# A hybrid decoder step on one core: order of the output projection's halves, and the first FFN run on unnormalised activations

## The chip, the cores and the metric

The kernel runs on one core of a Trainium2 chip. The metric is the device time of one execution in microseconds; the median of three runs is used. The span is what the hardware profiler records from the first instruction to the last. TensorE is called PE in the profile, VectorE DVE, ScalarE ACT, GpSimd POOL; SyncE (SP) issues the weight loads.

## What is computed

Two layers, each a pair of mixers (a Mamba-2 SSD and a Griffin RG-LRU) whose outputs are joined and projected back, followed by a SwiGLU channel mixer: dense in layer 0, eight experts in layer 1. The part that matters here, for 264 tokens (256 of a prompt and 8 samples) and a model width of 1024:

```python
x = x + jnp.concatenate([y_ssd, y_lru], axis=-1) @ P['w_out'][l]
hn = rmsnorm(x, P['ln_ffn'][l])          # x * rsqrt(mean(x*x) + EPS) * g
if l % 2 == 0:
    x = x + (jax.nn.silu(hn @ wg) * (hn @ wu)) @ wd      # D_FF = 2816
else:
    x = x + moe_swiglu(hn, ...)
```

## The kernel before, in words

Activations lie transposed: `xT` and `hn` hold 8 tiles of 128 features by 264 tokens, in f32. The program is written out by hand, one instruction list for each engine, with semaphores between them; nothing is scheduled by a compiler. A PSUM bank carries one output tile at a time. `plan_fills` (line 109) lays down at build time which bank each tile uses and as which fill of it; `begin(name)` on PE waits until the fill before it on that bank has been evicted, `done` counts the bank's `full` semaphore up, `filled` and `evacd` on ACT and DVE are its other side, and `evacuated` waits for an eviction.

Weights come as units of 1 MB (8 k-tiles by 256 columns, which is two output tiles) into a ring of six slots, `wring`. SP issues unit i when unit i-6 has been used. All products of the output projection and of the FFN run in split precision. ACT copies a unit as rounded high part to `fw_hi` (`high_weights`), DVE subtracts that and writes the low part `fw_lo` (`low_weights`, which signals `flo_ready`), and PE makes three products for each k-tile: high by high, low by high, high by low (`split_product`, 24 matmuls for one output tile of 8 k-tiles). There are two slots of `fw` (FSLOTS = 2), so ACT starts the high part of unit j+2 when PE is through with unit j (`unit_used`). The activations are split in the same manner, the mixers' output into `mix_hi` and `mix_lo`, the normalised `hn` into `hn_hi` and `hn_lo`.

The output projection has 8 units a layer, for 4 pairs of output tiles times 2 halves: half 1 multiplies the LRU's output, half 0 the SSD's. OUT_ORDER (line 87) is their order as (pair, half): (0,1), (1,1), (2,1), (0,0), (3,1), (1,0), (2,0), (3,0). I call these steps q0 to q7. A pair's LRU half comes first and opens its banks, its SSD half closes them. The eight output tiles use six banks, OUT_BANKS = (BA, BB, Q1, Q2, Q3, Q4): tiles 6 and 7 (pair 3) take the banks of tiles 0 and 1 (pair 0). In each step ACT waits for the step's unit to be used and makes the high part of the unit two on. DVE makes its low part and then, after an SSD half, adds the two output tiles into `xT` (`add_out`). ACT squares those for the norm (`out_squares`). In the last step DVE adds and ACT squares ahead of the weights.

Then, in both layers: PE sums the squares over the features with a matmul by a constant matrix (`mean_square`, 16 matmul records), ACT takes the square root (`rms`), DVE its reciprocal into `rs[:, 0]` and then x times gain times that (`normed`, 8 instructions), and in layer 0 ACT waits until the memory of the mixers' state is free (`ffn_region_free`), rounds `hn` to `hn_hi` (8 instructions) and DVE subtracts to `hn_lo` (8). The FFN loops over pairs of its 22 tiles, a gate unit (tiles `fg`) and an up unit (tiles `fu`) in turn, all on the two banks BA and BB: ACT evicts `fg` through Silu into `silu_t`, DVE evicts `fu` by multiplying the two into `rs[:, 1:3]`, ACT rounds that to `hid_hi` and DVE subtracts to `hid_lo`. The down projection (`fd`, 8 tiles, 16 units of 704 KB) closes the layer. Layer 1 then goes through the input projections and mixers again, and ends in the router and the experts, which take more than half of the span.

`hn_hi` lies in the memory that holds the low part of the LRU's mixer output, so it may only be written when the last LRU half of the output projection is done.

Of the kernel before, what the change touches and what calls it, by code (L numbers as in the profile page):

```python
# [23 lines left out]
F32 = mybir.dt.float32  # L24
# [8 lines left out]
KD = D // P  # L33
# [53 lines left out]
OUT_ORDER = ((0, 1), (1, 1), (2, 1), (0, 0), (3, 1), (1, 0), (2, 0), (3, 0))  # L87
# [23 lines left out]
def plan_fills():  # L111
# [12 lines left out]
    for l in range(LAYERS):  # L124
# [54 lines left out]
        if l == 0:  # L179
            for m in range(0, FT, 2):  # L180
                for kind in ("fg", "fu"):
                    for i in range(2):
                        tile(kind, m + i)
            for m in range(KD):
                tile("fd", m)
# [72 lines left out]
def trunk(nc, a, o):  # L258

    with ExitStack() as ctx:  # L260
# [233 lines left out]
        copies_out = sem("copies_out")  # L494
        hid_hi_ready = sem("hid_hi_ready")
# [339 lines left out]
        def _(pe):  # L835
# [154 lines left out]
            for l in range(LAYERS):  # L990
# [120 lines left out]
                for q, (pair, lru) in enumerate(OUT_ORDER):  # L1111
# [11 lines left out]
                    if lru:  # L1123
                        ins.then_inc(half_used, 1)
                mean_square(("ln_ffn", l), mean_d[:, :], [sq[:, m] for m in range(KD)],
                            lambda i: pe.wait_ge(sq_ready, 16 * l + 8 + i + 1))
                if l == 0:
                    for m in range(0, FT, 2):
                        for q, kind in enumerate(("fg", "fu")):
                            for i in range(2):  # L1130
# [4 lines left out]
                                     kind, m + i)  # L1135
                    for m in range(KD):
# [156 lines left out]
        def _(act):  # L1293
# [30 lines left out]
            for l in range(LAYERS):  # L1324
# [135 lines left out]
                for q, j in enumerate(OUT[l]):  # L1460
# [7 lines left out]

                    if q == len(OUT[l]) - 1:
                        out_squares()  # L1470
# [3 lines left out]
                    if not lru and q < len(OUT[l]) - 1:  # L1474
                        out_squares()
                    if q == 0:
                        high_parts(0, 4, XT)
                rms(("ln_ffn", l), 0)
                if l == 0:
                    ffn_region_free(act)  # L1480
                    for k in range(KD):
                        act.wait_ge(hn_ready, 8 + k + 1)
                        f(hn_hi[:, k], hn[:, k]).then_inc(hn_hi_ready, 1)
                    for i, j in enumerate(FFN):
                        w, last = UNITS[SPLIT[j]][0], UNITS[SPLIT[j]][5]
                        if w == "ffn_w_gate":
                            for m in (last[1] - 1, last[1]):
                                if m > 1:
                                    evacuated("fu", m - 2)
                                evacd(f(silu_t[:, m % 2, :], filled("fg", m)[:, 0:T], ACT.Silu), "fg", m)  # L1490
                        if i + FSLOTS < len(FFN):
                            unit_used(act, j)
                            high_weights(j + FSLOTS)
                        if w == "ffn_w_up":
                            for m in (last[1] - 1, last[1]):
                                evacuated("fu", m)
                                f(hid_hi[:, m, :], rs[:, 1 + m % 2, :]).then_inc(hid_hi_ready, 1)
# [103 lines left out]
        def _(dve):  # L1601
# [131 lines left out]
            for l in range(LAYERS):  # L1733
# [173 lines left out]
                for q, j in enumerate(OUT[l]):  # L1907
                    pair, lru = OUT_ORDER[q]

                    def add_out():  # L1910

                        for m in (2 * pair, 2 * pair + 1):
                            evacd(tt(xT[:, m, :], xT[:, m, :], filled("out", l, m)[:, 0:T], ALU.add), "out", l, m)

                    if q == len(OUT[l]) - 1:
                        add_out()
                    if j + FSLOTS < len(SPLIT):
                        low_weights(j + FSLOTS)
                    if not lru and q < len(OUT[l]) - 1:
                        add_out()  # L1920
                    if q == 0:
                        norm_parts(("ssd_norm", l, 1), 1, ysz, "ssd_norm", 4, XT)
                        low_parts(0, 4, XT)
                normed(("ln_ffn", l), l, "ln_ffn")
                if l == 0:
                    for k in range(KD):
                        dve.wait_ge(hn_hi_ready, k + 1)
                        tt(hn_lo[:, k], hn[:, k], hn_hi[:, k].bitcast(F32), ALU.subtract).then_inc(hn_lo_ready, 1)
                    for i, j in enumerate(FFN):
                        w, last = UNITS[SPLIT[j]][0], UNITS[SPLIT[j]][5]  # L1930
                        if w == "ffn_w_up":
                            for m in (last[1] - 1, last[1]):
                                evacuated("fg", m)
                                if m > 1:
                                    dve.wait_ge(hid_lo_ready, m - 1)
                                tt(rs[:, 1 + m % 2, :], silu_t[:, m % 2, :], filled("fu", m)[:, 0:T], ALU.mult
                                   ).then_inc(evac[fill("fu", m)[0]], 1)
# [207 lines left out]
```

## Time and profile before

| | us |
|---|---|
| median of 3 runs | 1835.09 (1833.96 to 1836.92) |
| the profiled execution | 1836.94 |
| its span | 1835.2 |
| PE busy | 1741.7 (95%) |
| DVE busy | 1356.3 (74%) |
| ACT busy | 1053.7 (57%) |
| PE's granted clock, mean | 0.976 |

The profiled execution's own time is 1.74 us more than its span. PE is the busiest engine and carries 83% of the chain that ended last. In the 40 slices of the page the stretches that matter here are slices 5 to 11 (layer 0's output projection from 223 us, its FFN from 289 to 488 us) and slices 16 and 17 (layer 1's output projection from 688 to 745 us). In a line of the timeline stand the start, the time taken, the engine, line, operation, names and count, and in brackets how long the engine was idle before it and who released it. Matmul ends are modelled and overlap the next start, so the step from one matmul to the next is read from starts. In a line of the stretches stand its bounds, its length, the busy time of PE, PEld (the weight load into PE), DVE, ACT and POOL, each with its count of instructions, and then the granted clock (1.00 is the level of 2.4 GHz, 0.50 that of 1.2 GHz), the DMA engines' busy share and GB/s.

### The profile page before, as it was taken

How to read it: one execution, taken by the hardware profiler on the slowest of the kernel's cores; microseconds unless marked ns; L12 is line 12 of the kernel's file. 1: busy time of each engine (PE TensorE's matmuls, PEld its weight loads, DVE VectorE, ACT ScalarE, POOL GpSimd, SP SyncE). 2: the span in 40 equal slices, each digit the busy share in tenths (PEclk: the TensorE clock that was granted, in tenths of full speed). 3: DMA queues.
4: the chain of work that ended last, by engine and by line, in shares of the span. 5: the costliest groups of instructions: out<-in, count | busy, mean ns of one | idle time of the engine just before them, and what ended most of it. 6: DMA issues, size and time to landing. Idle time of an engine off the chain costs nothing.

```text
span 1835.2 us, 24108 instructions
## 1 busy us (share of the span) xinstructions
PE 1741.7 (95%) x9024; PEld 1459.8 (80%) x9024; DVE 1356.3 (74%) x1335; ACT 1053.7 (57%) x1006; POOL 139.6 (8%) x135
## 2 busy tenths in 40 slices
PE   7999889999999988799999999999999999999995
PEld 5867788999887768778878788788788788787884
DVE  3668745554456775478888888888888888888885
ACT  2535434443242543366677776767776767776764
POOL 2056000000105420000000000000000000000000
PEclk9999999999999999799999999999999999999998
DMA  8455244555635425279999899899899899998991
GB/s 243 138 182 175 81 152 139 182 149 168 200 119 184 153 89 163 79 285 357 322 353 357 311 365 355 317 358 351 322 359 349 326 355 321 353 358 310 363 357 43
DMA packets 257028, 465.45 MB, mean 254 GB/s; under 512 B 8493, under 2 KB 108197, under 8 KB 256929
## 3 DMA queue, kind: packets, MB, share of 16 engines
q1 hardware_dynamic: 250288, 442.20, 69.9%
q0 software_dynamic: 6384, 21.28, 3.4%
q8 instruction: 42, 0.69, 0.2%
q10 hardware_dynamic: 288, 1.08, 0.2%
q14 instruction: 26, 0.21, 0.0%
HBM read 453.70 MB, written 11.15 MB: 253 GB/s over the span
## 4 chain that ended last, share of the span: by engine, by line
PE 83%; DVE 10%; ACT 2%; issue 2%; POOL 2%; DMA 1%; DVEq 0%; ACTq 0%; POOLq 0%
PE bank L851 80%; PE bank L855 2%; DVE arena L1624 2%; DVE arena L1627 2%; DVE w_lo L1627 1%; DVE moe_arena L1624 1%; ACT fw_hi L1307 1%; DVE fw_lo L1627 1%; DVE cs_t L1627 1%; ACT arena L1307 1%; DMA arena<-in_state_ssd 1%; POOL sam_tmp L740 1%; DVE arena L1829 0%; ACT w_hi L1307 0%; POOL sam_tmp L731 0%
## 5 line engine op out<-in xcount | busy, mean ns | idle before, releaser
L1627 DVE TENSOR_TENSOR w_lo<-wring,w_hi 128x2048 fp32r<-128x2048 f32 x336 | 768.3, 2291 | 118.0 <-ACT w_hi L1307 117.0
L1307 ACT ACTIVATE w_hi<-wring 128x2048 fp32r<-128x2048 f32 x336 | 643.6, 1918 | 254.3 <-PE bank L851 254.2
L851 PE MATMUL bank<-w_hi,xg_hi 128*128 128x512 f32 x896 | 359.8, 402 | 10.7 <-DVE w_lo L1627 9.0
L851 PE MATMUL bank<-w_lo,xg_hi 128*128 128x512 f32 x896 | 355.1, 396 | 0.0
L851 PE MATMUL bank<-w_hi,xg_lo 128*128 128x512 f32 x896 | 352.4, 393 | 0.0
L851 PE MATMUL bank<-hn,wring 128*128 128x264 f32 x1152 | 271.2, 393 | 6.2 <-DVE hn L1624 6.1
L851 PEld LDWEIGHTS bank<-hn,wring 128*128 128x128 f32 x1152 | 220.3, 193 | 50.2 <-issue 12.1
L1627 DVE TENSOR_TENSOR fw_lo<-wring,fw_hi 128x2048 fp32r<-128x2048 f32 (+1 forms) x54 | 113.1, 2095 | 132.8 <-ACT fw_hi L1307 132.8
L851 PEld LDWEIGHTS bank<-w_hi,xg_hi 128*128 128x128 f32 x896 | 168.3, 188 | 51.1 <-DVE w_lo L1627 12.6
L851 PEld LDWEIGHTS bank<-w_lo,xg_hi 128*128 128x128 f32 x896 | 168.2, 188 | 41.0
L851 PEld LDWEIGHTS bank<-w_hi,xg_lo 128*128 128x128 f32 x896 | 168.4, 188 | 38.7
L851 PE MATMUL bank<-w_hi,at_hi 128*128 128x512 f32 x448 | 178.4, 398 | 0.0
L851 PE MATMUL bank<-w_lo,at_hi 128*128 128x512 f32 x448 | 177.0, 395 | 0.0
L851 PE MATMUL bank<-w_hi,at_lo 128*128 128x512 f32 x448 | 175.9, 393 | 0.0
L1307 ACT ACTIVATE fw_hi<-wring 128x2048 fp32r<-128x2048 f32 (+1 forms) x54 | 94.9, 1758 | 111.7 <-PE bank L851 111.7
L1307 ACT ACTIVATE arena<-bank 128x11 f32<-128x11 f32 (+4 forms) x96 | 31.9, 349 | 177.5 <-PE bank L851 169.5
L1624 DVE SCALAR_TENSOR_TENSOR arena<-bank,par,arena 128x255 f32<-128x255 f32 (+2 forms) x120 | 57.6, 481 | 64.2 <-ACT arena L1307 61.2
L851 PEld LDWEIGHTS bank<-w_lo,at_hi 128*128 128x128 f32 x448 | 84.1, 188 | 21.1
L851 PEld LDWEIGHTS bank<-w_hi,at_lo 128*128 128x128 f32 x448 | 84.1, 188 | 20.2
L851 PEld LDWEIGHTS bank<-w_hi,at_hi 128*128 128x128 f32 x448 | 84.1, 188 | 19.2
L851 PE MATMUL bank<-hn_hi,fw_hi 128*128 128x264 f32 x352 | 88.5, 287 | 4.4 <-ACT hn_hi L1307 4.4
L851 PE MATMUL bank<-hn_hi,fw_lo 128*128 128x264 f32 x352 | 88.4, 286 | 0.0
(237 smaller groups left out, 2118.7 us busy)
## 6 DMA issues: line engine op xcount, KB each, us to landing
wring<-in_moe_w_gate SPq DMA_DIRECT2D x112, 1024.0 KB, 5.2
wring<-in_moe_w_up SPq DMA_DIRECT2D x112, 1024.0 KB, 5.2
wring<-in_moe_w_down SPq DMA_DIRECT2D x112, 1024.0 KB, 5.0
wring<-in_w_in SPq DMA_DIRECT2D x36, 1024.0 KB, 5.2
wring<-in_w_out SPq DMA_DIRECT2D x16, 1024.0 KB, 5.4
wring<-in_ffn_w_gate SPq DMA_DIRECT2D x11, 1024.0 KB, 5.4
wring<-in_ffn_w_up SPq DMA_DIRECT2D x11, 1024.0 KB, 5.3
wring<-in_ffn_w_down SPq DMA_DIRECT2D x16, 704.0 KB, 4.7
```

The costliest lines, as they stand in the source:

```text
L740: nc.gpsimd.tensor_tensor(prod, st, sam_c, ALU.mult).then_inc(prod_ready, 1)
L851: return nc.tensor.matmul(out, lhsT, rhs, start=start, stop=stop)
L855: return nc.tensor.transpose(out, in_, ident[0:k, 0:k])
L1307: return nc.scalar.activation(out, in_, fn, **kw)
L1624: return V.scalar_tensor_tensor(out=out, in0=in0, scalar=scalar, in1=in1, op0=op0, op1=op1)
L1627: return V.tensor_tensor(out, in0, in1, op)
```

## The change

Three edits. In both layers the order of the projection's steps q4 and q5 is exchanged: the SSD half of pair 1 now comes before the LRU half of pair 3. In layer 0 the FFN's gate and up products are fed with x times the norm's gain, without the division by the root mean square; that division is applied to each gate and up tile as DVE evicts it. In layer 0 the tiles of the FFN use the six banks in turn rather than two.

In detail, for layer 0: right behind each `add_out` DVE writes `hn` = xT times gain for the two tiles (8 `tensor_scalar` in place of 8 `scalar_tensor_tensor` behind the norm). ACT rounds them in pairs (`scaled_high`): pairs 0 and 1 in step (3,1), behind the weights and `ffn_region_free`; pair 2 in step (2,0); pair 3 in the last step ahead of the squares. DVE subtracts (`scaled_low`) pairs 0 and 1 in step (2,0), pair 2 in the last step ahead of its adds, pair 3 behind them. PE's `mean_square` stands behind the first gate tile. DVE evicts `fg` and `fu` with a multiplication by `rs[:, 0]`, ACT applies Silu in place in `silu_t`, and DVE multiplies the two. ACT makes the weights' high part ahead of its Silu rather than behind it. Layer 1 keeps its norm as it was.

The diff, without the new semaphores' declarations:

```diff
-OUT_ORDER = ((0, 1), (1, 1), (2, 1), (0, 0), (3, 1), (1, 0), (2, 0), (3, 0))
+OUT_ORDER = ((0, 1), (1, 1), (2, 1), (0, 0), (1, 0), (3, 1), (2, 0), (3, 0))
@@ plan_fills
             for m in range(0, FT, 2):
-                for kind in ("fg", "fu"):
+                for k, kind in enumerate(("fg", "fu")):
                     for i in range(2):
-                        tile(kind, m + i)
+                        pl.add(OUT_BANKS[(2 * m + 2 * k + i) % 6], kind, m + i)
             for m in range(KD):
-                tile("fd", m)
+                pl.add(OUT_BANKS[m % 6], "fd", m)
@@ tensor
-                mean_square(("ln_ffn", l), mean_d[:, :], [sq[:, m] for m in range(KD)],
-                            lambda i: pe.wait_ge(sq_ready, 16 * l + 8 + i + 1))
+                def ln_ffn():
+                    mean_square(("ln_ffn", l), mean_d[:, :], [sq[:, m] for m in range(KD)],
+                                lambda i: pe.wait_ge(sq_ready, 16 * l + 8 + i + 1))
+                if l == 1:
+                    ln_ffn()
...
                                 done(split_product(begin(kind, m + i), FFN[m + q], 0, KD, hn_hi, hn_lo, i * P, hi, ready),
                                      kind, m + i)
+                                if first:
+                                    ln_ffn()
@@ scalar
+                    def scaled_high(pair):
+                        for k in (2 * pair, 2 * pair + 1):
+                            act.wait_ge(hn_ready, 8 + k + 1)
+                            f(hn_hi[:, k], hn[:, k]).then_inc(hn_hi_ready, 1)
                     if q == len(OUT[l]) - 1:
+                        if l == 0:
+                            scaled_high(3)
                         out_squares()
                     if j + FSLOTS < len(SPLIT):
                         unit_used(act, j)
                         high_weights(j + FSLOTS)
                     if not lru and q < len(OUT[l]) - 1:
                         out_squares()
+                    if l == 0 and OUT_ORDER[q] == (3, 1):
+                        ffn_region_free(act)
+                        scaled_high(0)
+                        scaled_high(1)
+                    if l == 0 and OUT_ORDER[q] == (2, 0):
+                        scaled_high(2)
...
                 if l == 0:
-                    ffn_region_free(act)
-                    for k in range(KD):
-                        act.wait_ge(hn_ready, 8 + k + 1)
-                        f(hn_hi[:, k], hn[:, k]).then_inc(hn_hi_ready, 1)
                     for i, j in enumerate(FFN):
-                        if w == "ffn_w_gate":
-                            for m in (last[1] - 1, last[1]):
-                                if m > 1:
-                                    evacuated("fu", m - 2)
-                                evacd(f(silu_t[:, m % 2, :], filled("fg", m)[:, 0:T], ACT.Silu), "fg", m)
                         if i + FSLOTS < len(FFN):
                             unit_used(act, j)
                             high_weights(j + FSLOTS)
+                        if w == "ffn_w_gate":
+                            for m in (last[1] - 1, last[1]):
+                                evacuated("fg", m)
+                                f(silu_t[:, m % 2, :], silu_t[:, m % 2, :], ACT.Silu).then_inc(silu_ready, 1)
                         if w == "ffn_w_up":
-                                evacuated("fu", m)
+                                act.wait_ge(hid_ready, m + 1)
                                 f(hid_hi[:, m, :], rs[:, 1 + m % 2, :]).then_inc(hid_hi_ready, 1)
@@ vector, in add_out behind the two adds
+                        if l == 0:
+                            for m in (2 * pair, 2 * pair + 1):
+                                evacuated("out", l, m)
+                                V.tensor_scalar(hn[:, m, :], xT[:, m, :], col(l, PA, "ln_ffn", m), None, ALU.mult
+                                                ).then_inc(hn_ready, 1)
+                    def scaled_low(pair):
+                        for k in (2 * pair, 2 * pair + 1):
+                            dve.wait_ge(hn_hi_ready, k + 1)
+                            tt(hn_lo[:, k], hn[:, k], hn_hi[:, k].bitcast(F32), ALU.subtract).then_inc(hn_lo_ready, 1)
                     if q == len(OUT[l]) - 1:
+                        if l == 0:
+                            scaled_low(2)
                         add_out()
+                        if l == 0:
+                            scaled_low(3)
...
+                    if l == 0 and OUT_ORDER[q] == (2, 0):
+                        scaled_low(0)
+                        scaled_low(1)
...
-                normed(("ln_ffn", l), l, "ln_ffn")
+                if l == 1:
+                    normed(("ln_ffn", l), l, "ln_ffn")
                 if l == 0:
-                    for k in range(KD):
-                        dve.wait_ge(hn_hi_ready, k + 1)
-                        tt(hn_lo[:, k], hn[:, k], hn_hi[:, k].bitcast(F32), ALU.subtract).then_inc(hn_lo_ready, 1)
+                    evacuated("ln_ffn", l)
+                    link(V.reciprocal(rs[:, 0, :], rs[:, 0, :]))
                     for i, j in enumerate(FFN):
+                        if w == "ffn_w_gate":
+                            for m in (last[1] - 1, last[1]):
+                                if m > 1:
+                                    dve.wait_ge(hid_ready, m - 1)
+                                evacd(tt(silu_t[:, m % 2, :], filled("fg", m)[:, 0:T], rs[:, 0, :], ALU.mult), "fg", m)
                         if w == "ffn_w_up":
                             for m in (last[1] - 1, last[1]):
-                                evacuated("fg", m)
                                 if m > 1:
                                     dve.wait_ge(hid_lo_ready, m - 1)
-                                tt(rs[:, 1 + m % 2, :], silu_t[:, m % 2, :], filled("fu", m)[:, 0:T], ALU.mult
-                                   ).then_inc(evac[fill("fu", m)[0]], 1)
+                                evacd(tt(rs[:, 1 + m % 2, :], filled("fu", m)[:, 0:T], rs[:, 0, :], ALU.mult), "fu", m)
+                            for m in (last[1] - 1, last[1]):
+                                evacuated("fu", m)
+                                dve.wait_ge(silu_ready, m + 1)
+                                tt(rs[:, 1 + m % 2, :], rs[:, 1 + m % 2, :], silu_t[:, m % 2, :], ALU.mult
+                                   ).then_inc(hid_ready, 1)
```

## Rows read from the trace of the kernel before

**Rows 1.** The page of the kernel before: span, busy time and instructions of each engine

```profile
span 1835.2 us, 24108 instructions
...
PE 1741.7 (95%) x9024; PEld 1459.8 (80%) x9024; DVE 1356.3 (74%) x1335; ACT 1053.7 (57%) x1006; POOL 139.6 (8%) x135
```

**Rows 2.** Waits of PE, 223 to 289 us: in total, times, longest

```profile
PE bank L851 <- DVE xT L1627: 4.7, 1, 4.7
...
PE bank L851 <- ACT hn_hi L1307: 4.4, 1, 4.4
...
PE bank L851 <- DVE fw_lo L1627: 1.0, 1, 1.0
```

**Rows 3.** Timeline of PE, layer 0, steps q3 to q5

```profile
244.05 0.39 PE L851 MATMUL bank<-mix_hi,fw_hi 128*128 128x264 f32 x1 [1.04 <-DVE fw_lo L1627]
...
249.04 1.16 PE L851 MATMUL bank<-mix_lo,fw_hi 128*128 128x264 f32 x8
...
254.86 0.59 PE L851 MATMUL bank<-mix_hi,fw_hi 128*128 128x264 f32 x1 [4.67 <-DVE xT L1627]
...
260.31 0.31 PE L851 MATMUL bank<-mix_hi,fw_hi 128*128 128x264 f32 x1
```

**Rows 4.** Timeline of ACT, layer 0

```profile
250.23 1.91 ACT L1307 ACTIVATE fw_hi<-wring 128x2048 fp32r<-128x2048 f32 x1 [5.26 <-PE bank L851]
...
288.40 3.17 ACT L1307 ACTIVATE hn_hi<-hn 128x264 fp32r<-128x264 f32 x8 [3.33 <-DVE hn L1624]
...
303.41 1.92 ACT L1307 ACTIVATE fw_hi<-wring 128x2048 fp32r<-128x2048 f32 x1 [3.65 <-PE bank L851]
```

**Rows 5.** Timeline of DVE, layer 0

```profile
252.18 2.29 DVE L1627 TENSOR_TENSOR fw_lo<-wring,fw_hi 128x2048 fp32r<-128x2048 f32 x1 [4.88 <-ACT fw_hi L1307]
...
254.38 0.76 DVE L1627 TENSOR_TENSOR xT<-xT,bank 128x264 f32<-128x264 f32 x2
...
285.95 1.80 DVE L1667 RECIPROCAL rs<-rs 128x264 f32<-128x264 f32 x1
...
305.37 2.29 DVE L1627 TENSOR_TENSOR fw_lo<-wring,fw_hi 128x2048 fp32r<-128x2048 f32 x1 [1.45 <-ACT fw_hi L1307]
```

**Rows 6.** Timeline of PE, layer 0, from the norm to the second unit

```profile
280.82 3.72 PE L851 MATMUL bank<-arena,mean_d 128*128 128x264 f32 x16
...
288.96 0.56 PE L851 MATMUL bank<-hn_hi,fw_hi 128*128 128x264 f32 x1 [4.42 <-ACT hn_hi L1307]
...
297.36 0.28 PE L851 MATMUL bank<-hn_hi,fw_hi 128*128 128x264 f32 x1
```

**Rows 7.** Timeline of PE, layer 1, steps q3 to q5

```profile
713.83 1.16 PE L851 MATMUL bank<-mix_lo,fw_hi 128*128 128x264 f32 x8
...
719.65 0.59 PE L851 MATMUL bank<-mix_hi,fw_hi 128*128 128x264 f32 x1 [4.66 <-DVE xT L1627]
...
724.86 0.28 PE L851 MATMUL bank<-mix_hi,fw_hi 128*128 128x264 f32 x1
```

**Rows 8.** One line's instructions (L1752): duration in ns min/median/max, starts

```profile
L1752 DVE TENSOR_SCALAR dts<-dts,a_neg x2: 345/346/346, 58.1 to 524.7; 16x264 f32<-16x264 f32 x2
```

**Rows 9.** Timeline of POOL, its last transfer of layer 0's mixers

```profile
208.12 0.52 POOL L812 DMA_DIRECT2D out<-arena  x1
```

**Rows 10.** Busy time by stretch; behind POOL stand granted clock, DMA share, GB/s

```profile
250.10:260.20 10.10, 5.43 (x25) 5.34 (x25) 2.97 (x3) 2.68 (x3) 0.00 (x0) 0.67 0.52 172
...
289.00:298.00 9.00, 9.00 (x54) 9.00 (x55) 4.86 (x14) 4.68 (x11) 0.00 (x0) 0.70 0.19 66
...
493.00:494.00 1.00, 1.00 (x4) 0.79 (x3) 1.00 (x3) 0.00 (x0) 0.00 (x0) 0.50 0.83 340
...
786.00:788.00 2.00, 1.90 (x8) 1.58 (x9) 1.82 (x2) 0.00 (x0) 0.00 (x0) 1.00 0.95 379
```

**Rows 11.** Timeline of PE, two other gaps

```profile
491.52 8.82 PE L851 MATMUL bank<-hn,wring 128*128 128x264 f32 x31 [3.03 <-DVE hn L1624]
...
786.10 0.49 PE L851 MATMUL bank<-w_hi,xg_hi 128*128 128x512 f32 x1 [1.56 <-DVE xg_lo L1627]
```

More of the change, by code:

```diff
@@ L494, in trunk @@
         copies_out = sem("copies_out")
+        silu_ready = sem("silu_ready")
+        hid_ready = sem("hid_ready")
         hid_hi_ready = sem("hid_hi_ready")
```

## Prediction, written before the changed kernel ran

> **What bounds the kernel now.** First the page: PE is busy for 1741.7 of 1835.2 us [rows 1], so only PE's gaps and its slow stretches can be won, and an edit to ACT or DVE counts only where PE waits for it. Next the waits of PE around the changed code, 223 to 289 us. There are three: 4.7 us for DVE's add into `xT`, 4.4 us for ACT's `hn_hi`, and 1.0 us for a low part of weights [rows 2]. The timelines then show each gap and what follows it.
>
> The first gap: step q3 ends with eight matmuls from 249.04 that take 1.16 us, so PE could go on at about 250.02 by the step between starts, but it begins q4 at 254.86 [rows 3]. q4 was (3,1). Its tile 6 lies in the bank of tile 0, and tile 0 is evicted late, because DVE makes the low part of the next weights ahead of its adds. ACT starts the high part at 250.23, when the unit is used [rows 4], DVE the low part at 252.18, the adds at 254.38 [rows 5], and PE starts 0.05 us behind the first add's end. After the gap PE's granted clock is 0.50: the stretch from 250.10 to 260.20 has a mean of 0.67 [rows 10], and q4's first tile takes 260.31 - 254.86 = 5.45 us [rows 3]. A tile at full clock takes (280.82 - 260.31) / 7 = 2.93 us [rows 3, 6].
>
> The second gap: the norm's 16 matmul records run from 280.82 for 3.72 us; then PE waits 4.42 us, while ACT takes the root, DVE the reciprocal (1.80 us) and the first `hn`, and ACT the first `hn_hi` [rows 4 to 6]. PE starts the FFN at 288.96, and again behind a gap the clock is low, 0.70 over 289 to 298 us [rows 10]. The first up tile starts at 297.36 [rows 6].
>
> Layer 1 has the first gap once more: q3's last eight from 713.83, q4 at 719.65, its second tile at 724.86 [rows 7].
>
> **The exchanged order, both layers.** In the new order q4 is (1,0), whose banks are open and whose weights had been split during q2; PE waits for nothing. q5 is (3,1) and starts two tiles later, at 250.02 + 5.86 = 255.88. Tiles 0 and 1 are added by 254.38 + 0.76 = 255.14 [rows 5], 0.7 us before, and tile 0 already at 254.8. The weights of (3,1), made at 252.18 to 254.47, are ready as well. Later steps keep the old pattern: unit used, 1.91 us of ACT, 2.29 us of DVE, together with the hand-overs 4.45 us of the 5.86 us that a unit takes on PE. So no new wait follows. SP issues the two exchanged weight units in the other order, six units ahead; nothing is queued differently behind them, and POOL's list is untouched.
> Gain in layer 0: 254.86 - 250.02 = 4.84 us of gap and 5.45 - 2.93 = 2.52 us of slow clock, 7.36 us. In layer 1: free at 713.83 + 0.98 = 714.81, so 4.84 us, and 724.86 - 719.65 - 2.93 = 2.28 us; 7.12 us. The wait of 1.04 us ahead of q3 [rows 3] stays in both layers.
>
> **The norm behind the first gate tile, layer 0.** What is taken off PE's path is root, reciprocal and the gain's multiplication. What becomes late next is the last pair's add, since PE now wants `hn_hi` right behind q7. I follow it from PE's clock: q4 at 250.02, q5 at 255.88, q6 at 261.74, q7 at 267.60, all products done at 273.46.
> ACT learns that q6's unit is used about 0.2 us behind (250.23 against 250.02), so it makes the high part from 267.80 to 269.71, DVE the low part from 269.75, and the adds of pair 2 start 2.20 us later, at 271.95. From here DVE has a queue: two adds (step 0.34 us, from 0.76 us for two with 0.42 us for the last), two `tensor_scalar`, four subtractions of pairs 0 and 1, two of pair 2, then the add of tile 6. No row shows `tensor_scalar` on 128x264 from SBUF. The nearest is 346 ns for 264 elements with a pointer scalar [rows 8], on 16 partitions; overlapped like the others it is a step of 0.26 us. Its bounds are that and the add's 0.34 us step. I take 0.26. The sum is 2 x 0.34 + 2 x 0.26 + 6 x 0.34 = 3.24 us, so tile 6 is added from 275.2 to 275.65, and its bank, the first gate tile's, is free at 275.70. PE idles from about 273.6 to 275.70, 2.1 us; counted in starts the gap is 275.70 - 273.46 = 2.24 us (2.5 at the upper bound).
> The Trainium skill, "VectorE: DVE Perf Modes", section "The perf-mode tier table", has fp32 `tensor_scalar` from SBUF at twice the rate of `tensor_tensor`; the row of 346 ns beside 0.42 us agrees. Without that mode the gap would be the 2.5 us.
> ACT squares pair 2 and rounds it in time: eight roundings take 3.17 us [rows 4], 0.40 us each, behind two squares that take about as long each. Then tiles 6 and 7: `tensor_scalar` done at 276.25 and 276.5, `hn_hi` at 276.7 and 277.1, `hn_lo` at 277.2 and 277.6. PE asks for k-tile 6 of the high part 1.5 us after its start, at 277.2, and for the low parts at 277.7: no second wait, with 0.1 to 0.5 us to spare. Squares of tiles 6 and 7 end at 277.8, ahead of the norm's turn at 275.70 + 2.93 = 278.6. ACT's `ffn_region_free` now stands at 263.9 instead of behind the norm. It waits for transfers of which the last was issued at 208.12 [rows 9]; it costs nothing.
> PE's path from 250.02 to the first up tile is then 8 tiles of the projection (23.44), the gap (2.24), two gate tiles (5.86) and the norm (3.72): 35.26 us. Before it was 297.36 - 250.02 = 47.34 us. Gain 12.08 us, of which the exchange was 7.36 and the norm's move is 4.72: its gap goes from 4.42 to 2.24, and a slow start of 2.5 us goes.
>
> **Behind that, in the FFN.** The root ends at about 283, the reciprocal at 285, when the second gate tile is still on PE (it ends at 285.3). The gate tiles wait for eviction until then, which is what the six banks are for: PE may run six tiles before it needs BA again. ACT needs 1.3 us more for loading Silu's table, behind its weights; the first product is asked for four tiles later.
> In the steady loop DVE gets two more multiplications of 0.43 us per pair of tiles and kind, 44 in all, 19 us of work. They stand ahead of `fw_lo` in its list, so they count only if they are late. Before, ACT starts the up unit's high part at 303.41 and DVE the low part at 305.37, to 307.66 [rows 4, 5]; PE wants it at 297.36 + 4 x 2.93 = 309.08. So there is 1.4 us to spare, and about 2.0 us in which DVE waits for ACT anyway. The new work in front is the second `fu` eviction and two products behind it, with their waits 1.5 us: less than 2.0, cost nothing. ACT's Silu moves behind its weights and gives the gate unit's 0.3 us more. The down projection starts on BA, whose last gate or up tile (20) is evicted one tile before.
>
> **The sum.** 12.1 + 7.1 = 19.2 us. From the profiled execution's span 1835.2 this is 1816.0, with the 1.74 us around it 1817.7. The median of the runs stands 1.85 us below the profiled execution, so 1835.1 - 19.2 = 1815.9. I say 1816.0.
>
> **Rivals.**
> The clock falls in the new gap. The rows leave it open: an idle time of 3.03 us was followed by the low level (0.50 at 493 us), after 1.56 us it stayed at 1.00, and 2.1 us lies between [rows 10, 11]. PE had worked densely before both. A tile lost 2.3 to 2.5 us behind the old gaps [rows 3, 7]; a shorter stretch may cost half of it. So 1.2 to 2.5 us: 1817.2 to 1818.5. I give it 0.22, as the new gap is nearer to the short one.
> DVE's queue around q7 is longer than worked out, by its own hand-overs and by waits between ACT and DVE in turn (DVE waits for ACT's rounding of pair 2, ACT for DVE's products). Then the norm's move wins nothing, with a gap of over 4 us and a slow start as before, and only the exchange pays, 14.5 us: 1820.6. 0.08.
> Slower than before: the FFN becomes bound by DVE. The Trainium skill, same page, section "Rules for kernel authors", advises keeping the count of DVE operations small, and this change adds some 44. The mechanism here is `fw_lo` of the up unit held behind evictions and products. It decides from 2.0 + 1.4 = 3.4 us of DVE work behind the unit's end, against 1.5 us worked out. To turn 19 us into a loss, each of 11 pairs must lose over 1.7 us more, that is 5.1 us of DVE work in all; with 5.6 us the loss is 11 x 2.2 = 24 us, 1840. Against it: DVE idles 1.45 us even ahead of `fw_lo` now [rows 5]. 0.03.
> The exchange does not do what it says: PE waits at (3,1) or at another bank for as long as before, and the norm's new place only moves the 4.4 us. Then 1833 to 1836, no change. 0.03.
> The other side of the clock: slow stretches that follow later gaps (layer 1's start, the router) fall otherwise, as the places of PE's gaps shift in time. Each is worth up to 2.5 us either way; with two gained, below 1812.5. 0.04.
> The remaining 0.60 is the forecast, 1814 to 1817.5.
>
> **Range and chances.** 1812.5 to 1821.5 takes in the forecast, the fall of the clock and the lost norm move. About 0.2% (3.7 us) is what a measurement of this kernel can tell from no change. Faster by more: 0.60 + 0.22 + 0.08 + 0.04 = 0.94. Same 0.03, slower 0.03.
>
> **What would show it.** In the trace after: no idle time of PE between q3 and q7 in either layer, with full clock; a gap of about 2.1 us behind q7 of layer 0, released by DVE's add into `xT`; the norm's matmuls behind 24 of the FFN's and no wait behind them; no idle time of PE in the FFN; the first up tile 35 us behind q3's end. I am wrong if PE waits for `fw_lo` in the FFN, if the gap behind q7 is over 3 us, or if layer 1 gains less than 6 us.

## The result, and the profile after

The changed kernel takes 1819.39 us (median of 4 runs, 1817.82 to 1821.73), the kernel before 1835.49 in the same comparison. The ratio is 0.991, 95% interval 0.9897 to 0.9924: faster by 14 to 19 us. In a second comparison, beside 15 runs of the kernel before, it was 1818.98 and 0.9903 (0.9888 to 0.9918). The profiled execution took 1819.49 with a span of 1817.8 us. The forecast was 1816.0 with a range of 1812.5 to 1821.5.

From the page of the kernel after, to be held against [rows 1]: PE has 7 us less busy time for the same 9024 matmuls, nearly all of it in the two changed stretches, where it ran at the low clock less often. DVE has 15 us more, and the rest of the saving, 10 us, is idle time of PE that went.

```profile
span 1817.8 us, 24173 instructions
...
PE 1734.5 (95%) x9024; PEld 1453.0 (80%) x9024; DVE 1371.3 (75%) x1379; ACT 1052.1 (58%) x1006; POOL 139.5 (8%) x135
```

The waits of PE from 220 to 290 us. In [rows 2] there were three; the 4.7 us and the 4.4 us are gone, 1.0 us ahead of q3 stays, and 2.1 us is the new wait for the last pair's add:

```profile
PE bank L853 <- DVE xT L1645: 2.1, 1, 2.1
PE bank L853 <- DVE fw_lo L1645: 1.0, 1, 1.0
```

The timeline of PE, kernel after: q3 of layer 0, the first gate tile, the norm, the first up tile, layer 1's first projection, and in layer 1 q3 and the router's first matmul. They answer to [rows 3], [rows 6], [rows 7] and the first line of [rows 11].

```profile
243.13 0.39 PE L853 MATMUL bank<-mix_hi,fw_hi 128*128 128x264 f32 x1 [1.04 <-DVE fw_lo L1645]
...
274.79 0.39 PE L853 MATMUL bank<-hn_hi,fw_hi 128*128 128x264 f32 x1 [2.10 <-DVE xT L1645]
...
277.84 3.72 PE L853 MATMUL bank<-arena,mean_d 128*128 128x264 f32 x16
...
284.36 0.28 PE L853 MATMUL bank<-hn_hi,fw_hi 128*128 128x264 f32 x1
...
478.51 8.76 PE L853 MATMUL bank<-hn,wring 128*128 128x264 f32 x32 [3.03 <-DVE hn L1642]
...
697.33 0.39 PE L853 MATMUL bank<-mix_hi,fw_hi 128*128 128x264 f32 x1 [1.04 <-DVE fw_lo L1645]
...
736.27 10.38 PE L853 MATMUL bank<-w_router,hn 128*128 128x8 f32 x48 [5.82 <-issue]
```

Read from q3's start to the first up tile: 284.36 - 243.13 = 41.23 us, before 297.36 - 244.05 = 53.31 [rows 3, 6]. That is 12.08 us less. The DVE list that sets the new wait, which answers to [rows 5]:

```profile
268.83 2.29 DVE L1645 TENSOR_TENSOR fw_lo<-wring,fw_hi 128x2048 fp32r<-128x2048 f32 x1 [3.56 <-ACT fw_hi L1316]
271.04 0.76 DVE L1645 TENSOR_TENSOR xT<-xT,bank 128x264 f32<-128x264 f32 x2
271.72 0.62 DVE L1935 TENSOR_SCALAR hn<-xT,par 128x264 f32<-128x264 f32 x2
272.25 2.14 DVE L1645 TENSOR_TENSOR hn_lo<-hn,hn_hi 128x264 fp32r<-128x264 f32 x6
274.31 0.76 DVE L1645 TENSOR_TENSOR xT<-xT,bank 128x264 f32<-128x264 f32 x2
```

The first of the last two adds ends at 274.74 and PE starts at 274.79. PE's products of q7 ended about 272.7, when DVE had only just begun (at 272.25) with the six subtractions of `hn_lo` that stand ahead of the add.

A table of stretches, from starts of PE's matmuls in eight traces (us). "Before again" is a second trace of the kernel before; the others are the experiments below.

| trace | start to q3 | q3 to layer 1's first matmul | to q3 of layer 1 | to the router | to the end |
|---|---|---|---|---|---|
| before | 244.05 | 247.47 | 217.34 | 46.02 | 1080.32 |
| before again | 243.72 | 247.48 | 217.18 | 46.12 | 1080.40 |
| after | 243.13 | 235.38 | 218.82 | 38.94 | 1081.53 |
| after again | 245.64 | 235.36 | 218.91 | 38.94 | 1081.45 |
| order only | 241.98 | 240.37 | 217.54 | 38.94 | 1080.67 |
| norm only | 241.92 | 244.30 | 219.73 | 46.41 | 1081.14 |
| sum ahead | 241.59 | 234.36 | 219.67 | 38.94 | 1081.64 |
| adds first | 242.17 | 233.30 | 217.36 | 38.94 | 1081.53 |

The second and fourth column hold the changed code. After against before they give 12.1 and 7.1 us, 19.2 in all. The spans differ by 17.4: 0.9 us came ahead of q3, where the traces of unchanged code scatter from 241.59 to 245.64, 1.5 us was lost in layer 1's mixers and 1.2 us in the rest, in code that was not changed.

### The profile page after: what moved, and what is told of

Same layout as the page of the kernel before. It is cut to its first block, busy times and chain, and to the rows that moved or that the text cites. A ratio compares the mean times of both kernels' runs of the same rounds, so it can differ in the third digit from the quotient of the medians.

```text
span 1817.8 us, 24173 instructions
## 1 busy us (share of the span) xinstructions
PE 1734.5 (95%) x9024; PEld 1453.0 (80%) x9024; DVE 1371.3 (75%) x1379; ACT 1052.1 (58%) x1006; POOL 139.5 (8%) x135
## 4 chain that ended last, share of the span: by engine, by line
PE 83%; DVE 10%; ACT 2%; issue 2%; POOL 2%; DMA 1%; DVEq 0%; ACTq 0%; POOLq 0%
PE bank L853 81%; PE bank L857 2%; DVE arena L1642 2%; DVE arena L1645 2%; DVE w_lo L1645 1%; DVE moe_arena L1642 1%; DVE fw_lo L1645 1%; DVE cs_t L1645 1%; DMA arena<-in_state_ssd 1%; ACT fw_hi L1316 1%; ACT arena L1316 1%; POOL sam_tmp L742 1%; DVE arena L1847 0%; POOL sam_tmp L733 0%; DVE arena L1872 0%
```

## Experiments

**The changed kernel again, and the kernel before again.** No edit.

> The changed kernel once more, beside the kernel before on one chip. In the first pair of profiles the steps that the change touches gave 12.1 us in layer 0 and 7.1 us in layer 1, 19.2 us in all, but the spans differ by 17.4 us and the medians by 16.1 us. Theory: the rest is lost in code that was not changed, by slow stretches of PE's clock behind gaps that both kernels have, and that is chance; then the difference of medians over more runs lies between 16 and 19.5 us, and the two changed stretches again give 12.1 and 7.1 us. Rival: the changed kernel loses 2 to 3 us systematically in the unchanged stages; then the difference stays at 16 us with little scatter and the same stages lose again.

Measured: 1818.98 us against 1836.36. In the trace the changed stretches are the same to 0.02 us (table), and layer 1's mixers take 218.91 us. Both comparisons together, eight runs of the changed kernel have a mean of 1819.5; 15 of the kernel before have 1836.0. The difference is 16.5 us, at the low end of what the theory of chance allowed, and the mixers lost the same 1.5 us again, as the rival had it. This run doesn't tell the two apart.

> The kernel before once more, for a second trace of it. Measured from the first matmul of layer 1's input projection to step q3 of layer 1, code that no kernel here changes, the kernel before took 217.3 us and the order-only kernel 217.5 us, and the kernels with the norm's move 217.4 to 221.7 us, mostly 218.8 and more. Theory of chance: it depends on where PE's slow stretches fall, and the kernel before can give 219 to 220 us as well. Theory of a systematic loss: it is 217.3 to 217.6 us again.

Measured: 1836.58 us in its one run, and 217.18 us in layer 1's mixers, as the theory of a systematic loss had it. The trace of the padded kernel below speaks against it.

**Only the order.**

```diff
-OUT_ORDER = ((0, 1), (1, 1), (2, 1), (0, 0), (3, 1), (1, 0), (2, 0), (3, 0))
+OUT_ORDER = ((0, 1), (1, 1), (2, 1), (0, 0), (1, 0), (3, 1), (2, 0), (3, 0))
```

> The kernel before with only OUT_ORDER of the changed one: the exchange of steps q4 and q5 in both layers, norm and FFN as before. Theory: PE's wait of 4.7 us for DVE's add goes in both layers and the slow first tile behind it as well, 7.4 us in layer 0 and 7.1 in layer 1, so 14.5 us less than before, about 1821; the wait of 4.4 us ahead of the FFN stays as it was. Rival: the wait only moves to step (3,1) and the gain is under 4 us.

Measured: 1822.44 us, ratio 0.9921 (0.9907 to 0.9935), 13.9 us less. In the trace layer 1 gains 7.1 us and layer 0 also 7.1, with no wait of PE between q3 and q7; ahead of the FFN the old wait is there, and behind it the slow clock:

```profile
241.98 0.39 PE L851 MATMUL bank<-mix_hi,fw_hi 128*128 128x264 f32 x1 [1.04 <-DVE fw_lo L1627]
...
279.51 0.56 PE L851 MATMUL bank<-hn_hi,fw_hi 128*128 128x264 f32 x1 [4.42 <-ACT hn_hi L1307]
...
288.19 0.28 PE L851 MATMUL bank<-hn_hi,fw_hi 128*128 128x264 f32 x1
```

The exchange is most of the change, at the price worked out for it. Up to the FFN's first matmul layer 0 gains (288.96 - 244.05) - (279.51 - 241.98) = 7.38 us [rows 3, 6]. The first two gate tiles, still behind the old wait of 4.42 us, then take 8.68 us against 8.40 before, which makes it 7.1.

**Only the norm's move and the six banks.** The changed kernel with

```diff
-OUT_ORDER = ((0, 1), (1, 1), (2, 1), (0, 0), (1, 0), (3, 1), (2, 0), (3, 0))
+OUT_ORDER = ((0, 1), (1, 1), (2, 1), (0, 0), (3, 1), (1, 0), (2, 0), (3, 0))
...
                     if l == 0 and OUT_ORDER[q] == (3, 1):
                         ffn_region_free(act)
                         scaled_high(0)
+                    if l == 0 and OUT_ORDER[q] == (1, 0):
                         scaled_high(1)
```

> The changed kernel with the old OUT_ORDER (ACT rounds pair 1 in step (1,0), where its sum comes in this order): only the norm's move and the six banks are left of the change. Theory: PE's wait of 4.7 us in step (3,1) and its slow tile are back in both layers, and ahead of the FFN PE waits 2.1 us instead of 4.4 us, with full clock, so 4.7 us less than before, about 1831. Rival: without the exchange the rounding of pair 1 comes one step later and holds PE longer than 2.1 us behind q7; then the gain is under 3 us.

Measured: 1836.55 us (11 runs), ratio 1.0003 (0.9994 to 1.0012). Nothing is won, where 4.7 us were expected. Neither theory is right, since the wait has the length of the first:

```profile
252.72 0.59 PE L853 MATMUL bank<-mix_hi,fw_hi 128*128 128x264 f32 x1 [4.66 <-DVE xT L1646]
...
281.02 0.39 PE L853 MATMUL bank<-hn_hi,fw_hi 128*128 128x264 f32 x1 [2.15 <-DVE xT L1646]
```

But here the clock falls behind the gap, which it did not in the changed kernel. Two stretches, the first of this kernel and the second of the kernel after, each of 8 us around the start of the FFN; the granted clock is the third number from the end:

```profile
280.00:288.00 8.00, 6.98 (x35) 6.64 (x36) 4.91 (x9) 3.17 (x5) 0.00 (x0) 0.79 0.24 84
```

```profile
272.00:280.00 8.00, 5.90 (x40) 5.39 (x39) 5.81 (x15) 4.06 (x8) 0.00 (x0) 1.00 0.42 133
```

With a mean of 0.79 over 8 us, 6.98 of them busy, the slow time costs (1 - 0.79) x 8 = 1.7 us. The gain in the second column of the table is 3.17 us. The third column then is 2.4 us longer than before, and the last 0.8 us. So in this trace the gain is given back behind the changed code. Against the kernel before, PE is idle there for just as long and has more slow clock, as in the stretch from the gap ahead of layer 1's gate products to its state transposes (this kernel, then the kernel before):

```profile
586.88:651.73 64.85, 57.98 (x264) 43.12 (x265) 49.84 (x71) 31.82 (x54) 37.27 (x26) 0.92 0.46 156
```

```profile
591.83:655.31 63.48, 56.59 (x265) 42.15 (x265) 49.87 (x71) 31.82 (x54) 37.30 (x26) 0.96 0.48 159
```

This is not one execution's accident. The mean granted clock of the 11 runs of this kernel is 0.9740, of the 15 runs of the kernel before beside them 0.9751. One minus that, times the span, is 47.7 us of lost clock against 45.7: on average 2.0 us more, with an error of 0.5 us. What the shorter gap saves is given back as slow clock.

**The norm's sum ahead of the first gate tile.** The changed kernel with

```diff
-                if l == 1:
-                    ln_ffn()
+                ln_ffn()
...
-                                if first:
-                                    ln_ffn()
```

> The changed kernel with the norm's matmuls ahead of the first gate tile, as before, while the FFN still takes x times gain. This takes the place behind the tile from the change and keeps the late division. Theory: PE begins the 16 matmuls of the norm right behind q7, in the time in which it now waits 2.1 us, waits some 1 us for the squares of tiles 6 and 7 instead, and is 1.0 to 1.3 us earlier at the second gate tile: 1 us faster than the changed kernel. Rival, the reason for which one would put it behind: the squares are so late that PE loses more than the 2.1 us; then it is slower than the changed kernel by 1 us or more.

Measured: 1818.45 us, 0.9905 (0.989 to 0.992), 0.5 us less than the changed kernel beside it, whose interval overlaps. The trace decides. PE does 12 of the norm's 16 matmuls in the gap and waits 1.12 us for the squares; the second column of the table is 1.0 us shorter.

```profile
270.99 2.83 PE L853 MATMUL bank<-arena,mean_d 128*128 128x264 f32 x12
274.94 1.16 PE L853 MATMUL bank<-arena,mean_d 128*128 128x264 f32 x4 [1.12 <-ACT arena L1313]
```

So the place behind the first tile brings nothing. What pays in the trace is that the products no longer need the norm.

**Two banks for the FFN.** The changed kernel with

```diff
-                        pl.add(OUT_BANKS[(2 * m + 2 * k + i) % 6], kind, m + i)
+                        tile(kind, m + i)
...
-                pl.add(OUT_BANKS[m % 6], "fd", m)
+                tile("fd", m)
```

> The changed kernel with its FFN tiles on the two banks BA and BB, as before, instead of six. Theory of the prediction: PE may only run past the second gate tile because six banks are there. But by the changed kernel's trace DVE evicts the first gate tile at 283.95 to 284.38 and PE wants its bank again at 284.36, and in the loop each tile is evicted over 0.4 us before its bank is asked for. So: the same time as the changed kernel, within 0.5 us by the trace. Rival: PE waits at each pair for an eviction that stands behind the low part of the weights on DVE, 1 us for each of 11 pairs or more, 10 us slower.

Measured: 1819.15 us, 0.9905 (0.9888 to 0.9922). From the first gate tile to layer 1's first matmul it is 479.77 - 275.86 = 203.91 us against 203.72, with no wait of PE between. The six banks are not needed. This trace is also the one that loses most in code that was not changed: layer 1's mixers take 701.45 - 479.77 = 221.68 us in it, 4.3 more than before.

**DVE's adds first around q7.** The changed kernel with

```diff
                     if q == len(OUT[l]) - 1:
-                        if l == 0:
-                            scaled_low(2)
                         add_out()
                         if l == 0:
+                            scaled_low(2)
                             scaled_low(3)
+                    if l == 0 and OUT_ORDER[q] == (2, 0):
+                        scaled_low(0)
+                        scaled_low(1)
                     if j + FSLOTS < len(SPLIT):
                         low_weights(j + FSLOTS)
                     if not lru and q < len(OUT[l]) - 1:
                         add_out()
-                    if l == 0 and OUT_ORDER[q] == (2, 0):
-                        scaled_low(0)
-                        scaled_low(1)
```

> The changed kernel with DVE's list around q7 reordered in layer 0: the subtractions of pairs 0 and 1 ahead of the low part of the weights in step (2,0), where DVE is idle for 3.6 us, and those of pair 2 behind the adds of tiles 6 and 7. Theory: the wait of 2.1 us ahead of the FFN is DVE's queue and nothing else; tile 6 is now added right behind pair 2's, PE waits 0.2 us instead of 2.1, and the kernel is 1.9 to 2 us faster than the changed one. Rival: PE then waits for hn_hi or hn_lo of tiles 6 and 7 instead, and under 1 us is won.

Measured: 1818.04 us, 0.9903 (0.9886 to 0.9919); in the trace 235.38 - 233.30 = 2.08 us, the whole wait. The median lies only 0.9 to 1.4 us below the two of the changed kernel, with intervals of 3 us either way, so the trace alone shows the gain. DVE's list now has the adds directly behind pair 2's:

```profile
270.07 0.76 DVE L1645 TENSOR_TENSOR xT<-xT,bank 128x264 f32<-128x264 f32 x2
270.75 0.62 DVE L1935 TENSOR_SCALAR hn<-xT,par 128x264 f32<-128x264 f32 x2
271.29 0.91 DVE L1645 TENSOR_TENSOR xT<-xT,bank 128x264 f32<-128x264 f32 x2
```

The wait was DVE's queue, as worked out, and four of the six subtractions could stand where DVE is idle.

**The SSD's second half behind the weights of q1.** The changed kernel with, on ACT,

```diff
-                    if q == 0:
+                    if q == 1:
                         high_parts(0, 4, XT)
```

and on DVE

```diff
                         norm_parts(("ssd_norm", l, 1), 1, ysz, "ssd_norm", 4, XT)
-                        low_parts(0, 4, XT)
+                    if q == 1:
+                        low_parts(0, 4, XT)
```

> The changed kernel with the rounding and subtraction of the second half of the SSD's output moved one step back, from q0 to behind the weights of q1, on ACT and DVE, in both layers. Theory: the wait of 1.04 us ahead of q3 comes from the weights of q3, which stand behind that rounding on ACT; it goes in both layers, 1.2 us each by the step between starts, 2.3 us faster than the changed kernel. Rival: PE then waits in q3 for the rounded output itself and nothing is won.

Measured: 1816.66 us, 0.989 (0.9873 to 0.9907), 2.3 to 2.7 us below the changed kernel's two medians, where 2.3 were expected; the intervals overlap. The wait of 1.04 us ahead of q3 is gone in both layers. From q0 of layer 1 to the router it is 735.79 - 677.46 = 58.33 us against 736.27 - 676.57 = 59.70.

**Both.**

> The changed kernel with both of these: DVE's adds first around q7, and the SSD's second half behind the weights of q1. Theory: PE runs from q0 of layer 0 to the end of its FFN without a wait of over 0.3 us, and from q0 of layer 1 to its norm as well; 4.2 us faster than the changed kernel, about 1815, in the profile and, within 1.5 us, in the medians. If only the profile's stretches show it and the median moves less than 2.5 us, then time is given back in the unchanged stages, as the norm's move did by itself.

Measured: 1816.61 us, 0.9892 (0.9875 to 0.9909). From q0 of layer 0 to layer 1's first matmul the trace has 476.30 - 223.56 = 252.74 us against 478.51 - 222.35 = 256.16, 3.4 us less, and PE has no wait of over 0.2 us in it. Layer 1 gives 1.3 us more. The median moves by 2.4 to 2.8 us, though, no more than with the second edit alone. With four runs each and intervals of 3 us either way, the two can't be told apart. The 4.2 us that were expected are in the stretches and not in the median. It is the fastest version here with the previous one.

**Padding.** The kernel before with, on DVE in each pair of tiles of layer 0's FFN,

```diff
+                            for n in range(8):
+                                dve.wait_ge(consts_ready, n + 1)
```

> The kernel before with 88 waits on DVE in layer 0's FFN that are met long before, eight for each pair of tiles: nothing is computed otherwise, only DVE's instruction list is longer. Theory: what the norm's move loses in unchanged code (about 2 us in layer 1's mixers and 0.65 us in the experts' last part, where PE waits 4.2 us rather than 3.9 for DVE) comes with a longer list of instructions, by the place at which later code lies; then this kernel has 4.2 us in that wait and is 1 to 2.7 us slower than before. Rival: the loss belongs to the norm's move itself or to chance; then all stages are as before, 3.9 us in that wait, and the time is within 0.7 us of before.

Measured: 1835.92 us (11 runs), 0.9995 (0.9986 to 1.0004). The wait in the experts' last part stays at 3.9 us. The length of the list is not the cause of the longer wait. But its trace gives layer 1's mixers 710.16 - 490.26 = 219.90 us, 2.6 to 2.7 us more than the two traces of the kernel before, in an execution that was the slowest of its 11 (1839.38). So the mixers can take 219.9 us without the norm's move, and 217.2 is not their fixed time.

**One and two reciprocals more in each up unit.** The changed kernel with `link` around each, and 1 or 2 for N:

```diff
+                        if w == "ffn_w_up":
+                            for _ in range(N):
+                                link(V.reciprocal(rs_x[:, :], rs[:, 0, :]))
```

> The changed kernel with one more reciprocal (1.8 us, result unused) on DVE in each up unit of layer 0's FFN, behind the products and ahead of the weights' low part: 11 of them, 20 us more work for DVE. Theory of the prediction: DVE may be late by 3.4 us behind the end of the unit before PE notices; the list behind it is now 1.1 us of evictions and products plus 1.8, so PE waits for nothing and the FFN's length (from its first matmul to the next layer's first) is as in the changed kernel within 0.3 us. Rival: DVE is already the bound of the FFN; then each pair takes 1.8 us more, 20 us in all.

Measured: 1817.78 us in its one run. DVE has 20 us more to do and PE has no wait in the gate and up units, as the theory had it. The FFN is 477.90 - 273.32 = 204.58 us long, 0.9 more where at most 0.3 was expected. One wait of 0.63 us stands at the start of the down projection, where a unit takes PE less time (4.0 us against 5.86) and DVE's low part of the weights stands behind the last extra reciprocal.

> The same with two reciprocals in each up unit, 3.6 us, 4.8 us in all behind the unit's end. Theory: that is 1.3 us over the cover of 3.4 us, so PE waits 1.2 to 1.5 us for fw_lo in each of 11 pairs, 13 to 17 us in all, and the kernel comes out at about 1833 to 1836, as the kernel before: the slower rival's price per pair is right, and the change is 3.7 us of DVE work per pair away from it. Rival: other waits follow it (hid_lo, silu), or PE's clock falls in each of them, and it is above 1845.

Measured: 1839.64 us, 1.0018 (1.0008 to 1.0027) of the kernel before, so about 3 us slower than it, and above the 1833 to 1836 that were expected. PE's waits in the FFN, and one of them:

```profile
PE bank L854 <- DVE fw_lo L1646: 16.4, 11, 2.5
...
313.20 0.36 PE L854 MATMUL bank<-hn_hi,fw_hi 128*128 128x264 f32 x1 [1.39 <-DVE fw_lo L1646]
```

From 299.86 to 313.20 a pair takes 13.34 us instead of 11.7, 1.6 us more for a wait of 1.4, and behind the longest wait, 2.47 us at the start of the down projection, the granted clock is 0.55 for the next 3.8 us. The FFN is 501.51 - 277.13 = 224.38 us, 20.7 more. The mechanism is the one that the prediction named for "slower than before". The price of 13 to 17 us was too low, by a fifth at its upper end.

## Why the prediction held, and where it was off

- The exchanged order. 7.36 and 7.12 us were worked out. The order-only kernel's trace has 7.38 up to the FFN (7.1 with the slower gate tiles behind it) and 7.1, and its median 13.9 of 14.5 us. What I said of the later steps, that none of them waits, shows in every trace with this order.
- The norm's move. The new gap was worked out as 2.1 us of idle time, released by the add of tile 6, and measured as 2.10 by that add. The `tensor_scalar` on 128x264, for which only a row of 16 partitions was there, takes 0.62 us for two, a step of 0.27 us against 0.26. The Trainium skill, "VectorE: DVE Perf Modes", section "The perf-mode tier table", gives it twice the rate of `tensor_tensor`; here one takes 0.35 us against 0.42, which fits that, though one size doesn't show the rate. The upper bound was added up wrong, with no effect: at 0.34 us a step the gap is 2.40 us, not 2.5. No second wait follows. The path from q3's end to the first up tile came out 12.08 us shorter, as summed. That it fits to the hundredth is in part luck, since the gate tiles behind the old gap alone differ by 0.28 us between two traces. Against the order-only trace the norm's move gives 240.37 - 235.38 = 5.0 us, where 4.72 were worked out.
- The FFN. By starts, the up unit's products end 1.4 us behind the unit's end (302.54 + 0.77 against 301.92 in the lines below), near the 1.5 worked out, and PE never waits for `fw_lo`. The slower rival stayed away, and the reciprocals show that its point was well placed: one more in each unit costs 0.9 us in all, two more turn the change into a loss. That the six banks are what lets PE run past the norm was wrong. With two banks PE's wait would be the time from 284.36 to the first gate tile's eviction at 284.38; the second gate tile is on PE for as long as root and reciprocal take.

```profile
301.92 0.28 PE L853 MATMUL bank<-hn_hi,fw_hi 128*128 128x264 f32 x1
```

```profile
302.19 0.43 DVE L1645 TENSOR_TENSOR rs<-bank,rs 128x264 f32<-128x264 f32 x1 [1.34 <-PE bank L853]
302.54 0.77 DVE L1645 TENSOR_TENSOR rs<-rs,silu_t 128x264 f32<-128x264 f32 x2
```

- The clock in the new gap. It stayed at 1.00 in both of the changed kernel's traces and in four of its variants (2.10 or 2.11 us of idle time), and fell in the norm-only kernel's one trace, with 2.15 us. The rival with chance 0.22 is real. The one trace in which it came true is also the only one that has this gap behind the old order, and whether it belongs to that order or to the single execution isn't shown.
- The sum. The forecast was 3.4 us too low, inside the range: 19.2 us of gain were forecast and 16.1 measured between the medians. No term of the changed stretches is at fault. The step that was off is the silent one, that code behind the change keeps its time. The kernels with the norm's move all have a wait of 4.2 us for DVE in the experts' last part where the kernel before, its padded form and the order-only kernel have 3.9; from the first expert matmul to the end (786.10 us in [rows 11]) they take 1049.66 to 1049.85 us, the others 1049.14 to 1049.43. The rest falls in layer 1's mixers: 218.82 to 219.73 us in four of the five traces of the table with the norm's move, 221.68 in the two-banks trace and 218.4 and 218.6 in two more, against 217.34 before. Three traces with the move lose nothing there: adds first (217.36), both edits (217.54) and one reciprocal (217.59). The whole stretch, in the trace before, after, norm only and two banks:

```profile
491.52:708.86 217.34, 204.65 (x1041) 164.91 (x1041) 147.42 (x251) 93.69 (x174) 60.02 (x47) 0.97 0.44 143
```

```profile
478.51:697.33 218.82, 205.49 (x1040) 165.53 (x1040) 147.44 (x251) 93.60 (x174) 60.00 (x47) 0.96 0.44 142
```

```profile
486.22:705.95 219.73, 206.71 (x1041) 166.33 (x1041) 147.38 (x251) 93.61 (x174) 59.94 (x47) 0.95 0.42 142
```

```profile
479.77:701.45 221.68, 208.29 (x1041) 167.43 (x1041) 147.41 (x251) 93.61 (x174) 59.95 (x47) 0.95 0.42 140
```

The work is the same and the time PE doesn't work grows by at most 0.7 us (12.69 to 13.39), while its busy time goes from 204.65 to 208.29 us as the granted clock falls from 0.97 to 0.95. So most of what is lost there is slow clock. The padded kernel, without the norm's move, has 219.90 us at 0.95.

What stays open: why the norm's move brings only 2.3 us in the means behind the exchange (1821.8 against 1819.5, with an error of over 1 us) and nothing by itself, where the stretches give 5.0 and 3.2. The clocks of the runs show what the second is given back in, 2.0 us of slow clock on average, and the norm-only trace shows some of it in code that was not changed. Why PE gets the low clock there more often, no run here shows, and neither does any show why the wait in the experts' last part is 0.3 us longer: a longer instruction list alone doesn't do it. The mixers' code is the same in all traces, and their time scatters from 217.2 to 221.7 us. That ACT now makes the weights' high part ahead of its Silu was not tested by itself.

## What to carry to other kernels

When a bank's second user stands directly behind its first, look whether a step with other banks can go between; one line paid 14 us here, a third of it through the clock (7.1 us for each gap of 4.7), since the gap slowed the matmuls behind it. A wait that hangs on an in-order engine is shortened by moving what nobody needs yet out of its way: four subtractions to where DVE is idle and two behind the adds were worth 2 us in the trace. And a gain of 2 us on a path of 1800 that has other gaps may not be found again in the median, so read it in its stretch and say so.

## What was not expected of the hardware

The granted clock's answer to a gap is not fixed by the gap. The idle time of 3.03 us ahead of layer 1's projection was followed by the low level in the trace before [rows 10, 11], and in the kernel with the adds first it was not (nor in the one with one reciprocal, while in the other twelve traces it was), with PE busy for the whole stretch at 1.00:

```profile
475.50:485.50 10.00, 10.00 (x45) 7.17 (x46) 5.55 (x13) 2.97 (x6) 0.00 (x0) 1.00 0.37 129
```

In the kernel after the same stretch has 0.86:

```profile
478.50:488.50 10.00, 9.99 (x38) 7.55 (x39) 4.63 (x12) 1.81 (x5) 0.00 (x0) 0.86 0.25 95
```

And 2.15 us was enough once. Behind this one gap of 3.03 us the slow stretch costs 1.4 us in the trace above, (1 - 0.86) x 10, and 3.1 us in the two-banks trace, whose first 10 us have a mean of 0.69. Executions of one kernel differ by up to 7.5 us (1832.35 to 1839.85 for the kernel before, in 21 runs).
